# Decayed attention of the last branch: two heads per unit, one unit ahead

## The chip, the cores and the metric

The kernel runs on one core of a Trainium2 chip. The time is that of one execution on the device, in microseconds (us), as the median of several runs. A profile shows one execution, engine by engine: PE is TensorE (PEld its weight loads), DVE the vector engine, ACT the scalar engine, POOL GpSimd, SP the queue that issues most DMAs. The granted clock of TensorE is given as a share of its full 2.4 GHz.

## What is computed

A two-layer block with convolution, state-space and linear attention, cross attention and MLPs is followed by a second block on 512 tokens of width 1024. That second block has three attention branches (a: differential, b: sliding window, c: decayed or "forgetting"), each gated by a projection `gm` and projected up by `w_up`; the sum goes through `w_o` and a last norm. Only branch c is touched. Cut to what matters:

```python
def forgetting_attention(q, k, v, logf):          # S = 512, H = 8, d = 64, nb = 4 blocks of 128 queries
    c = jnp.cumsum(logf, axis=1)
    def one_block(args):
        qblk, cblk, start = args
        s = jnp.einsum('bqhd,bkhd->bhqk', qblk, k) * scale
        decay = jnp.transpose(cblk, (0, 2, 1))[:, :, :, None] - c_k[:, :, None, :]
        s = jnp.where((dist >= 0)[None, None], s + decay, -jnp.inf)
        p = jax.nn.softmax(s, axis=-1)
        return jnp.einsum('bhqk,bkhd->bqhd', p, v)

qc, kc, vc, fc, gc, gm = ...                      # columns of h @ w_in
uc = jnp.einsum('bse,ed->bsd', yc * jax.nn.silu(gc), w_up_c)
merged = gates[:, :, 0] * ua + gates[:, :, 1] * ub + gates[:, :, 2] * uc
out = rms_norm(x + merged @ w_o)
```

## The kernel before, in words

The program is written by hand, engine by engine: each engine has one list of instructions in program order, and semaphores join the lists. Nothing reorders them. Products of the large gemms are made as three products of rounded halves (`product3`, lines 596 to 598), so each step over 128 rows of weights is three records of 128x512. Weights stream through `raw`, are split by ACT into `w_hi` (L1336) and by DVE into `w_lo` (L2157), in four slots.

**Units.** Attention of each branch runs in units. In branches a and b a unit holds two maps (64 rows of `QK` at partitions 0 to 63 and 64 to 127). In branch c a unit is one head `hd` and one block `t` of 128 queries, 32 units; it has (t+1)*128 keys, so its row is 128, 256, 384 or 512 wide. For each unit:

- PE makes the scores (`scores_c`, L1269: 64 rows, (t+1)*128 columns, one product, two records);
- DVE adds the running decay sums of keys and queries (`maxima`, L2860), adds the causal mask on the last block (L2864) and takes the row maximum (L2865);
- ACT takes the exponential and the row sum (`exps`, L2045);
- PE transposes the weights (`turns_c`, L728, one record per 128x128 block), ACT copies them out (L2092), PE multiplies by the values (`values_c`, L1282, 64 columns, two records per block), DVE scales and gates the result (L2901).

**Key sums.** The decay sums of a head's keys are spread over partitions by four transposes on PE (`key_sums`, L728 reading `sm`), and DVE copies them negated (L2918). A head's sums are made in unit 1 of the head before.

**What sets the order.** Function `units` (PE) issues, for a unit n: in c and b the transposes of n, the scores of n+2 (`AHEAD` = 2), steps of the gate projection `gm` as filling (`gate_products`: 64 steps over the whole branch, eight of them before the first unit, the rest spread evenly), and the values product of n. In a (`AHEAD` = 1) the order is scores of n+1, half of the steps, transposes of n, the other half, values of n. DVE goes through reciprocal (L2884), maxima of n+2, at times one weight split, values of n, at times key sums. ACT goes through the copy of n's transposes, the exponentials of n+2, at times a copy of a finished gate chunk (L2072) and a weight split.

**Banks.** Everything but the gemms goes through four PSUM banks `paux`, taken in turn by a fixed list (`aux_plan`): entry number a can only be written when entry a-4 has been read (`next_aux`, `free_aux`). So the order in that list sets who waits for whose reader.

After the 32 units the output of the branch is transposed (`turned_output`), and the gemms `up_c` and `w_o` and the last norm follow; they need all of it.

## Time and profile before

| | us |
|---|---|
| median of 3 runs | 2392.0 (2391.42 to 2392.83) |
| the profiled execution | 2392.23 |
| its span | 2390.5 |
| PE busy | 2280.9 |
| DVE busy | 1312.0 |
| ACT busy | 914.6 |
| DMA, mean rate over the span | 94 GB/s |

The span is what the profile covers of the execution; some 1.7 us lie around it. Busy times of matmul records overlap a little (a record is longer than the distance to the next), so distances are read from start to start in the timeline. Branch c's units lie between 2196 and 2315 us, branch a's, used for comparison, between 1833 and 1907 us.

### The profile page before, as it was taken

Reading aid. Unit: us, or ns where it says so; the run is one execution under the profiler, and the core shown is the slowest. Engines: PE = TensorE matmul, PEld = TensorE weight load, DVE = VectorE, ACT = ScalarE, POOL = GpSimd, SP = SyncE. Lnnn points to the kernel's source line nnn. Section 1 sums busy time; section 2 is a strip of 40 time slices with the busy share of each in tenths; the row PEclk is TensorE's granted clock in tenths of the full one; section 3 lists DMA queues with packets and bytes.
Section 4 is the critical chain, followed back from the end, with each engine's and each line's share of the span. In section 5 each row is a group of like instructions: output and inputs, shape, how many; then the busy total and the mean of one; then the engine's idle time right before and its main releaser. Section 6 shows DMA issues by size and latency. Waiting matters only on the chain.

```text
span 2390.5 us, 27557 instructions
## 1 busy us (share of the span) xinstructions
PE 2280.9 (95%) x11120; PEld 1862.9 (78%) x11120; DVE 1312.0 (55%) x1946; ACT 914.6 (38%) x1636; POOL 164.2 (7%) x115
## 2 busy tenths in 40 slices
PE   7997889999999999999899999999899899999898
PEld 5886677877888888888787778888777688877677
DVE  4997798754833334735564573333533734622564
ACT  3353564342423323334334332232334534523353
POOL 0000300040400000400003040000000000000000
PEclk9998999999999999999899999999989999999999
DMA  5222224423333232321232223332222232122113
GB/s 164 88 88 74 86 93 176 145 80 124 116 106 106 88 106 89 115 71 54 80 141 71 88 91 113 99 106 89 88 106 88 54 88 71 54 88 88 36 36 115
DMA packets 180021, 224.68 MB, mean 94 GB/s; under 512 B 16603, under 2 KB 139174, under 8 KB 178870
## 3 DMA queue, kind: packets, MB, share of 16 engines
q1 hardware_dynamic: 167632, 191.90, 25.2%
q10 hardware_dynamic: 11686, 22.62, 2.7%
q0 software_dynamic: 576, 8.39, 0.9%
q8 instruction: 89, 1.46, 0.3%
q14 instruction: 38, 0.31, 0.0%
HBM read 213.72 MB, written 9.18 MB: 93 GB/s over the span
## 4 chain that ended last, share of the span: by engine, by line
PE 84%; DVE 11%; ACT 2%; issue 2%; POOL 1%; ACTq 1%; DVEq 0%
PE gemm L596 25%; PE gemm L597 24%; PE gemm L598 24%; PE aux L728 2%; DVE w_lo L2157 1%; DVE y_plain L2363 1%; PE aux L971 1%; PE aux L993 1%; PE aux L1269 1%; DVE x_lo L2180 1%; DVE work L2295 1%; POOL work L528 1%; PE aux L1282 1%; PE aux L1239 0%; PE aux L1086 0%
## 5 line engine op out<-in xcount | busy, mean ns | idle before, releaser
L596 PE MATMUL gemm<-x_hi,w_hi 128*128 128x512 f32 x1288 | 518.4, 402 | 6.1 <-DVE w_lo L2157 3.7
L598 PE MATMUL gemm<-x_hi,w_lo 128*128 128x512 f32 x1288 | 504.0, 391 | 0.0
L597 PE MATMUL gemm<-x_lo,w_hi 128*128 128x512 f32 x1288 | 504.0, 391 | 0.0
L2157 DVE TENSOR_TENSOR w_lo<-raw,w_hi 128x1024 fp32r<-128x1024 f32 x222 | 284.7, 1304 | 283.2 <-ACT w_hi L1336 282.4
L1336 ACT ACTIVATE w_hi<-raw 128x1024 fp32r<-128x1024 f32 x222 | 228.4, 1054 | 280.9 <-PE gemm L598 277.8
L596 PE MATMUL gemm<-w_hi,y_hi 128*128 128x512 f32 (+1 forms) x832 | 320.8, 386 | 0.0
L597 PE MATMUL gemm<-w_lo,y_hi 128*128 128x512 f32 (+1 forms) x832 | 317.6, 382 | 0.0
L2153 DVE TENSOR_TENSOR w_lo<-raw,w_hi 128x1024 fp32r<-128x1024 f32 x140 | 168.4, 1222 | 268.8 <-ACT w_hi L1334 259.4
L596 PEld LDWEIGHTS gemm<-x_hi,w_hi 128*128 128x128 f32 x1288 | 243.3, 189 | 82.8 <-issue 24.2
L598 PE MATMUL gemm<-w_hi,y_lo 128*128 128x512 f32 x768 | 299.5, 390 | 0.0
L598 PEld LDWEIGHTS gemm<-x_hi,w_lo 128*128 128x128 f32 x1288 | 243.0, 189 | 52.0
L597 PEld LDWEIGHTS gemm<-x_lo,w_hi 128*128 128x128 f32 x1288 | 243.3, 189 | 47.1 <-issue 1.0
L1334 ACT ACTIVATE w_hi<-raw 128x1024 fp32r<-128x1024 f32 x140 | 144.7, 1054 | 251.8 <-PE gemm L598 246.8
L596 PE MATMUL gemm<-w_hi,x_hi 128*128 128x512 f32 (+2 forms) x640 | 224.7, 351 | 2.1 <-issue 2.1
L597 PE MATMUL gemm<-w_lo,x_hi 128*128 128x512 f32 (+2 forms) x640 | 220.5, 344 | 0.0
L598 PE MATMUL gemm<-w_hi,x_lo 128*128 128x512 f32 (+2 forms) x640 | 220.1, 344 | 0.0
L596 PEld LDWEIGHTS gemm<-w_hi,y_hi 128*128 128x128 f32 x832 | 157.0, 189 | 31.5 <-issue 1.7
L597 PEld LDWEIGHTS gemm<-w_lo,y_hi 128*128 128x128 f32 x832 | 156.8, 189 | 31.6 <-issue 1.7
L598 PEld LDWEIGHTS gemm<-w_hi,y_lo 128*128 128x128 f32 x768 | 144.6, 188 | 30.2
L2363 DVE SCALAR_TENSOR_TENSOR y_plain<-work,par,y_plain 128x512 f32<-128x512 f32 x217 | 148.9, 745 | 4.3 <-ACT y_plain L1540 3.9
L596 PEld LDWEIGHTS gemm<-w_hi,x_hi 128*128 128x128 f32 x640 | 123.0, 192 | 21.9 <-issue 6.9
L597 PEld LDWEIGHTS gemm<-w_lo,x_hi 128*128 128x128 f32 x640 | 123.0, 192 | 14.4 <-issue 0.2
(327 smaller groups left out, 2788.3 us busy)
## 6 DMA issues: line engine op xcount, KB each, us to landing
raw<-in_mlp_w_dram SPq DMA_DIRECT2D x64, 1024.0 KB, 5.4
raw<-in_w_in_dram SPq DMA_DIRECT2D x31, 1024.0 KB, 5.1
raw<-in_odd_w_in_dram SPq DMA_DIRECT2D x12, 1024.0 KB, 5.2
raw<-in_even_w_in_dram SPq DMA_DIRECT2D x10, 1024.0 KB, 4.9
raw<-in_even_w_in_dram SPq DMA_DIRECT2D x16, 512.0 KB, 5.2
raw<-in_xa_w_k_dram SPq DMA_DIRECT2D x8, 1024.0 KB, 5.1
raw<-in_xa_w_v_dram SPq DMA_DIRECT2D x8, 1024.0 KB, 5.1
raw<-in_even_w_out_dram SPq DMA_DIRECT2D x8, 1024.0 KB, 4.9
```

Source lines behind the costliest of these rows:

```text
L528: pool.tensor_scalar(DIAG[:, i % 3, :], ident[:, :], par_col("even_conv_w", i * KC + KC - 1), None, ALU.mult).then_inc(S["diag_ready"], 1)
L596: pe.matmul(dst, a_hi, b_hi, start=first, stop=False)
L597: pe.matmul(dst, a_hi, b_lo, start=False, stop=False)
L598: return pe.matmul(dst, a_lo, b_hi, start=False, stop=last)
L728: return pe.transpose(dst, src, ident[0:src.shape[0], 0:src.shape[0]])
L971: ins = pe.matmul(dst[:, t2 * MEM:(t2 + 1) * MEM], XQ[:, 2 * hd + d, t * P:(t + 1) * P], KT[:, 2 * hd + d, :], start=(d == 0), stop=(d == 1))
L993: ins = pe.matmul(dst[:, :], VM[:, m, j * P:(j + 1) * P], PTX[:, m, hd, :], start=(m == 0), stop=(m == 1))
L1334: act.activation(piece(w_hi, s), raw_piece(n, s % 2), ACT.Copy).then_inc(w_hi_ready, 1)
L1336: act.activation(w_hi[:, s % W_SLOTS, :, :], raw[:, n % RAW_SLOTS, :, (s % 2) * P:(s % 2 + 1) * P], ACT.Copy).then_inc(w_hi_ready, 1)
L2153: dve.tensor_tensor(piece(w_lo, s), raw_piece(s // 2, s % 2), piece(w_hi, s).bitcast(F32), ALU.subtract).then_inc(w_lo_ready, 1)
L2157: dve.tensor_tensor(w_lo[:, s % W_SLOTS, :, :], raw[:, s // 2 % RAW_SLOTS, :, half], w_hi[:, s % W_SLOTS, :, :].bitcast(F32), ALU.subtract)\
L2363: ins = dve.scalar_tensor_tensor(U[:, f, CONV_W - 1:] if last else acc, U[:, f, i:i + T], par_col("even_conv_w", i * KC + f), acc, ALU.mul ...
```

## The change

A unit of branch c now holds two heads `(pr, t)`, 2*pr and 2*pr+1, so there are 16 units of two maps. The two score products of a unit are issued one behind the other on rows 0 to 63 and 64 to 127. Branch c takes the order of branch a: one unit of scores ahead, half of the steps ahead of the transposes and half behind. The transposes of both maps take a bank each, and ACT copies each on its own; the odd units' copies go to `y_plain`. On DVE the adds stay two, while the mask, the maximum and the reciprocal cover both maps in one instruction each; the values step has two writes. Key sums of the next pair's two heads are made behind the values product of units 0 and 1, and are kept in `y_plain` (`KEY_SUMS`), four heads at a time. The gate steps are still 64, eight before the first unit, 3.5 on average in each unit. Branches a and b keep their instructions.

```diff
-AHEAD = dict(a=1, b=2, c=2)
+AHEAD = dict(a=1, b=2, c=1)
...
-            if name == "C" and u[1] == 1 and u[0] + 1 < 8:
-                out += [("cb_c", u[0] + 1)]
             turns = [(name, "T", u, j) for j in range(nt)]
             scores = [(name, "S", us[n + ahead], j) for j in range(ns)] if n + ahead < len(us) else []
             out += turns + scores if ahead == 2 else scores + turns
             if pv:
                 out += [(name, "PV", u)]
+            if name == "C" and u[1] < 2 and u[0] + 1 < 4:
+                out += [("cb_c", 2 * u[0] + 2 + u[1])]
...
-    e += [("fc_rows",), ("fc",), ("cc",), ("cb_c", 0)]
-    e += units("C", [(hd, t) for hd in range(8) for t in range(TT)], 1, 1, True) + [("Ct", j) for j in range(4)]
+    e += [("fc_rows",), ("fc",), ("cc",), ("cb_c", 0), ("cb_c", 1)]
+    e += units("C", [(pr, t) for pr in range(4) for t in range(TT)], 2, 2, True) + [("Ct", j) for j in range(4)]
...
-            return (EX[:, 0, 0, :], EX[:, 1, 0, :], EX[:, 0, 1, :] if b == "b" else NC)[unit_slot(b, u)]
+            return (EX[:, 0, 0, :], EX[:, 1, 0, :], EX[:, 0, 1, :])[unit_slot(b, u)]
+
+        KEY_SUMS = y_plain[:, 2048:4096].rearrange("p (a b) -> p a b", b=T)
+
+        def pair_weights(u, g):
+
+            return PT[:, g, :] if UNIT[("C", u)] % 2 == 0 else y_plain[:, T * g:T * g + T]
...
-                    before(u)
-                    if b == "a":
+                    if b != "b":
                         if n + 1 < len(us):
                             scores(us[n + 1])
                         gate_products(b, (gate_steps(b, n - 1, len(us)) + gate_steps(b, n, len(us))) // 2)
+                    if b == "a":
                         pe.wait_ge(S["p_ready"], UNIT[(name, u)] + 1)
                     else:
                         pe.wait_ge(S["unit_exp"], UNIT[(name, u)] - 2 * TT + 1)
-                    turns(u, next_aux(name, "T", u, 0)).then_inc(aux_done, 1)
-                    if b != "a" and n + 2 < len(us):
+                    for g in range(2 if b == "c" else 1):
+                        turns(u, next_aux(name, "T", u, g), g).then_inc(aux_done, 1)
+                    if b == "b" and n + 2 < len(us):
                         scores(us[n + 2])
                     gate_products(b, gate_steps(b, n, len(us)))
-                    aux_read(pe, name, "T", u, 0)
+                    for g in range(2 if b == "c" else 1):
+                        aux_read(pe, name, "T", u, g)
                     values(u, next_aux(name, "PV", u)).then_inc(aux_done, 1)
+                    after(u)
                 gate_products(b, KC * KC)
                 at["gate"] = 0
                 at["panel"] += 4
...
             def scores_c(u):
-                hd, t = u
-                a = 64 * (hd % 2)
-                pe.matmul(next_aux("C", "S", u, 0)[:, 0:(t + 1) * P], QK[a:a + 64, hd // 2, t * P:(t + 1) * P],
-                          QK[a:a + 64, 4 + hd // 2, 0:(t + 1) * P], start=True, stop=True).then_inc(aux_done, 1)
-
-            def turns_c(u, dst):
-                row = unit_row("c", u)
+                pr, t = u
+                for g in range(2):
+                    a = 64 * g
+                    pe.matmul(next_aux("C", "S", u, g)[:, 0:(t + 1) * P], QK[a:a + 64, pr, t * P:(t + 1) * P],
+                              QK[a:a + 64, 4 + pr, 0:(t + 1) * P], start=True, stop=True).then_inc(aux_done, 1)
+
+            def turns_c(u, dst, g):
+                e = unit_slot("c", u)
                 for kt in range(u[1] + 1):
-                    ins = turn(dst[:, kt * P:(kt + 1) * P], row[:, kt * P:(kt + 1) * P])
+                    ins = turn(dst[:, kt * P:(kt + 1) * P], EX[:, e, g, kt * P:(kt + 1) * P])
                 return ins
 
             def values_c(u, dst):
-                hd, t = u
-                e = UNIT[("C", u)] % 2
-                for kt in range(t + 1):
-                    ins = pe.matmul(dst[:, 0:64], PT[:, e, kt * P:(kt + 1) * P], BV[:, kt, hd * 64:(hd + 1) * 64],
-                                    start=(kt == 0), stop=(kt == t))
+                pr, t = u
+                for g in range(2):
+                    s = slice((2 * pr + g) * 64, (2 * pr + g) * 64 + 64)
+                    for kt in range(t + 1):
+                        ins = pe.matmul(dst[:, 64 * g:64 * g + 64], pair_weights(u, g)[:, kt * P:(kt + 1) * P],
+                                        BV[:, kt, s], start=(kt == 0), stop=(kt == t))
                 return ins
...
-                    if b == "a":
+                    if b != "b":
                         for m in range(2):
                             v = EX[:, e, m, 0:(t + 1) * P]
...
+                    if b == "c":
+                        free_aux(act.activation(pair_weights(u, 0)[:, 0:(u[1] + 1) * P], bank[:, 0:(u[1] + 1) * P],
+                                                ACT.Copy), (B, "T", u, 0))
+                        bank = wait_aux(act, (B, "T", u, 1))
+                        src, dst = bank[:, 0:(u[1] + 1) * P], pair_weights(u, 1)[:, 0:(u[1] + 1) * P]
+                    elif b == "b":
...
-                        row = unit_row(b, u)
-                        bank = wait_aux(dve, ("C", "S", u, 0))
-                        free_aux(dve.scalar_tensor_tensor(row[:, 0:n], EX[:, hd % 2, 1, 0:n],
-                                                          sm[:, 4 + t, hd:hd + 1], bank[:, 0:n], ALU.add, ALU.add),
-                                 ("C", "S", u, 0))
+                        for g in range(2):
+                            bank = wait_aux(dve, ("C", "S", u, g))
+                            free_aux(dve.scalar_tensor_tensor(EX[:, e, g, 0:n], KEY_SUMS[:, 2 * (hd % 2) + g, 0:n],
+                                                              sm[:, 4 + t, 2 * hd + g:2 * hd + g + 1], bank[:, 0:n],
+                                                              ALU.add, ALU.add), ("C", "S", u, g))
                         aux_read(dve, "C", "S", u, 0)
-                        step(dve.tensor_tensor(row[:, n - P:n], row[:, n - P:n], R[:, 0:P], ALU.add))
-                        ins = dve.tensor_reduce(mxs[:, e, 0:1], row[:, 0:n], AX.X, ALU.max, negate=True)
+                        aux_read(dve, "C", "S", u, 1)
+                        last = EX[:, e, :, n - P:n]
+                        step(dve.tensor_tensor(last, last, over(R[:, 0:P], 2), ALU.add))
+                        ins = dve.tensor_reduce(mxs[:, e, 0:2], EX[:, e, :, 0:n], AX.X, ALU.max, negate=True)
...
-                        s = slice(64 * hd, 64 * hd + 64)
-                        ins = dve.scalar_tensor_tensor(YT[:, t, s], bank[:, 0:64], rs[:, e, 2:3], BG[:, t, s],
-                                                       ALU.mult, ALU.mult)
+                        for g in range(2):
+                            s = slice(128 * hd + 64 * g, 128 * hd + 64 * g + 64)
+                            ins = dve.scalar_tensor_tensor(YT[:, t, s], bank[:, 64 * g:64 * g + 64],
+                                                           rs[:, e, 2 + g:3 + g], BG[:, t, s], ALU.mult, ALU.mult)
...
-                    free_aux(dve.tensor_scalar(EX[:, hd % 2, 1, :], bank[:, :], -1.0, None, ALU.mult), ("cb_c", hd))
+                    free_aux(dve.tensor_scalar(KEY_SUMS[:, hd % 4, :], bank[:, :], -1.0, None, ALU.mult), ("cb_c", hd))
...
                 if b == "c":
                     key_sums(0)
+                    key_sums(1)
                 for u in us[:AHEAD[b]]:
                     maxima(u)
                 for n, u in enumerate(us):
-                    weights(u)
+                    if b != "c":
+                        weights(u)
                     if n + AHEAD[b] < len(us):
                         maxima(us[n + AHEAD[b]])
+                    if b == "c":
+                        weights(u)
                     if n:
                         split_chunks(2 * FIRST_PANEL[f"gm_{b}"] + W_SLOTS + gate_steps(b, n - 1, len(us)) // KC)
                     values(u, u == us[-1])
                     if b == "a" and n:
                         gated(n - 1)
-                    if b == "c" and u[1] == 1 and u[0] + 1 < 8:
-                        key_sums(u[0] + 1)
+                    if b == "c" and u[1] < 2 and u[0] + 1 < 4:
+                        key_sums(2 * u[0] + 2 + u[1])
```

What stands in PE's list, before, in the second head: the scores of its unit of 384 columns, one step of the gate, the values product of its unit of 128, the four transposes of the next head's key sums (`ident,sm`), the transposes of its unit of 256 and the scores of its unit of 512.

```order
L1269 MATMUL aux<-work 128x384 [waits aux_free2]
L596 MATMUL gemm<-x_hi,w_hi 128x512
L597 MATMUL gemm<-x_lo,w_hi 128x512
L598 MATMUL gemm<-x_hi,w_lo 128x512
L1282 MATMUL aux<-work 128x64 [waits aux_free3,aux_free1]
L728 MATMUL aux<-ident,sm 128x128 [waits aux_free0]
L728 MATMUL aux<-ident,sm 128x128 x3
L728 MATMUL aux<-ident,work 128x128 [waits aux_free1,unit_exp]
L728 MATMUL aux<-ident,work 128x128
L1269 MATMUL aux<-work 128x512 [waits aux_free2]
```

After, in PE's list at the first pair: the key sums, the two score products of 512 columns, one step, and the transposes of both maps of the unit of 384.

```order
L734 MATMUL aux<-ident,sm 128x128 [waits aux_free0]
L734 MATMUL aux<-ident,sm 128x128 x3
L1279 MATMUL aux<-work 128x512 [waits aux_free1]
L1279 MATMUL aux<-work 128x512 [waits aux_free2]
L602 MATMUL gemm<-x_hi,w_hi 128x512
L603 MATMUL gemm<-x_lo,w_hi 128x512
L604 MATMUL gemm<-x_hi,w_lo 128x512
L734 MATMUL aux<-ident,work 128x128 [waits aux_free3,unit_exp]
L734 MATMUL aux<-ident,work 128x128 x2
L734 MATMUL aux<-ident,work 128x128 [waits aux_free0]
L734 MATMUL aux<-ident,work 128x128 x2
```

Key sums no longer stand right ahead of transposes; the scores come in twos, and a step of the gate stands between scores and transposes.

DVE's list before, where key sums are read: weight split, values, key-sum copy, reciprocal, then the adds, mask and maximum of a unit.

```order
L2157 TENSOR_TENSOR w_lo<-raw,w_hi 128x1024 [waits w_hi_ready]
L2901 SCALAR_TENSOR_TENSOR work<-aux,rs,work 128x64 [waits aux_done]
L2918 TENSOR_SCALAR work<-aux 128x512 [waits aux_done]
L2884 RECIPROCAL rs<-rs 128x1 [waits unit_exp,aux_free3]
L2860 SCALAR_TENSOR_TENSOR work<-work,sm,aux 128x128 [waits aux_done,dve_step]
L2864 TENSOR_TENSOR work<-work 128x128 [waits aux_free0]
L2865 TENSOR_REDUCE mxs<-work 128x1 [waits dve_step]
```

After, at the pair's unit with 512 columns: weight split, the two values writes, key-sum copy, the adds of both maps, then mask and maximum once for both.

```order
L2171 TENSOR_TENSOR w_lo<-raw,w_hi 128x1024 [waits w_hi_ready,dve_step]
L2918 SCALAR_TENSOR_TENSOR work<-aux,rs,work 128x64 [waits aux_done]
L2918 SCALAR_TENSOR_TENSOR work<-aux,rs,work 128x64
L2935 TENSOR_SCALAR y_plain<-aux 128x512 [waits aux_done]
L2874 SCALAR_TENSOR_TENSOR work<-y_plain,sm,aux 128x512 [waits aux_done,aux_free0]
L2874 SCALAR_TENSOR_TENSOR work<-y_plain,sm,aux 128x512 [waits aux_done]
L2880 TENSOR_TENSOR work<-work 128x2x128 [waits aux_free2,aux_free1]
L2881 TENSOR_REDUCE mxs<-work 128x2 [waits dve_step]
L2900 RECIPROCAL rs<-rs 128x2 [waits unit_exp]
```

The reciprocal, which waits for the exponentials of the unit, now stands behind the maximum of the next unit.

## Rows read from the trace of the kernel before

**Rows 1.** The page: span, and the busy times of engines.
```profile
span 2390.5 us, 27557 instructions
...
PE 2280.9 (95%) x11120; PEld 1862.9 (78%) x11120; DVE 1312.0 (55%) x1946; ACT 914.6 (38%) x1636; POOL 164.2 (7%) x115
```
**Rows 2.** Timeline of PE in branch c: start us, us, line, out<-in, count [idle before].
```profile
2196.25 1.09 PE L728 MATMUL aux<-ident,sm 128*128 128x128 f32 x4 [0.28 <-DVE sm L2826]
...
2252.80 1.12 PE L1269 MATMUL aux<-work 64*128 64x512 f32 x2
2253.85 0.50 PE L596 MATMUL gemm<-x_hi,w_hi 128*128 128x512 f32 x1
...
2256.97 0.52 PE L728 MATMUL aux<-ident,work 128*128 128x128 f32 x3 [1.07 <-DVE work L2918]
...
2258.63 0.39 PE L596 MATMUL gemm<-x_hi,w_hi 128*128 128x512 f32 x1
...
2259.32 0.78 PE L1282 MATMUL aux<-work 128*128 128x64 f32 x6
2259.94 0.61 PE L728 MATMUL aux<-ident,work 128*128 128x128 f32 x4
...
2265.49 0.60 PE L728 MATMUL aux<-ident,sm 128*128 128x128 f32 x4
2265.93 0.38 PE L728 MATMUL aux<-ident,work 128*128 128x128 f32 x2
...
2313.51 1.00 PE L1282 MATMUL aux<-work 128*128 128x64 f32 x8
```
**Rows 3.** Waits of PE in branch c, then branch a: us, times, longest us.
```profile
PE aux L728 <- DVE work L2918: 9.2, 7, 2.0
...
PE aux L728 <- DVE work L2878: 4.0, 3, 1.3
```
**Rows 4.** Windows of branch c: length, PE, PEld, DVE, ACT, POOL busy, PEclk, DMA share, GB/s.
```profile
2196.20:2203.00 6.80, 6.75 (x18) 4.91 (x19) 5.28 (x11) 1.09 (x4) 0.00 (x0) 0.51 0.45 137
2230.60:2234.20 3.60, 3.60 (x15) 2.86 (x13) 0.41 (x3) 1.02 (x3) 0.00 (x0) 0.55 0.37 131
```
**Rows 5.** Timeline of PE in branch a.
```profile
1863.56 1.13 PE L1191 MATMUL aux<-work 64*128 64x512 f32 x4
1864.62 0.50 PE L596 MATMUL gemm<-x_hi,w_hi 128*128 128x512 f32 x1
...
1870.96 0.66 PE L728 MATMUL aux<-ident,work 128*128 128x128 f32 x4 [1.32 <-DVE work L2878]
...
1881.29 1.13 PE L1191 MATMUL aux<-work 64*128 64x512 f32 x4
```
**Rows 6.** Windows of the score lines alone, PE and PEld busy, c then a.
```profile
2196.20:2314.60 118.40, 26.29 (x64) 9.88 (x64) 0.96 0.11 36
...
1833.00:1905.00 72.00, 12.96 (x64) 4.82 (x64) 1.00 0.14 44
```
**Rows 7.** Timeline of DVE: branch a, then branch c.
```profile
1865.58 1.28 DVE L2839 SCALAR_TENSOR_TENSOR work<-work,aux 128x512 f32<-128x512 f32 x2
1866.89 1.22 DVE L2842 TENSOR_REDUCE mxs<-work 128x2 f32<-128x1024 f32 x1
...
2251.90 0.29 DVE L2864 TENSOR_TENSOR work<-work 128x128 f32<-128x128 f32 x1
...
2255.94 0.28 DVE L2901 SCALAR_TENSOR_TENSOR work<-aux,rs,work 128x64 f32<-128x64 f32 x1
2256.14 0.68 DVE L2918 TENSOR_SCALAR work<-aux 128x512 f32<-128x512 f32 x1
```
**Rows 8.** Timeline of ACT: branch a, then branch c.
```profile
1868.14 0.72 ACT L2035 ACTIVATE work<-work,mxs 128x512 f32<-128x512 f32 x1 [1.29 <-DVE mxs L2842]
...
1869.48 0.19 ACT L2035 ACTIVATION_READ_ACCUMULATOR work<-work,mxs 128x1 f32 x1
...
2260.58 0.60 ACT L2092 ACTIVATE work<-aux 128x512 f32<-128x512 f32 x1 [1.05 <-PE aux L728]
```

More of the change, by code:

```diff
@@ L206 @@
          + [("B", (hd, t)) for hd in range(4) for t in range(TT)]
-         + [("C", (hd, t)) for hd in range(8) for t in range(TT)])
+         + [("C", (pr, t)) for pr in range(4) for t in range(TT)])
 UNIT = {key: n for n, key in enumerate(UNITS)}
@@ L1144, in gate_products, with units @@
                     at["gate"] += 1
-            def units(b, us, scores, turns, values, before=lambda u: None):
+            def units(b, us, scores, turns, values, after=lambda u: None):
                 name = b.upper()
@@ L1192, in scores_a, with turns_a @@
                               QK[a:a + 64, 4 + hd, 0:(t + 1) * P], start=True, stop=True).then_inc(aux_done, 1)
-            def turns_a(u, dst):
+            def turns_a(u, dst, g):
                 e = UNIT[("A", u)] % 2
@@ L1223, in scores_b, with turns_b @@
                               QK[a:a + 64, 4, lo_key:(t + 1) * P], start=True, stop=True).then_inc(aux_done, 1)
-            def turns_b(u, dst):
+            def turns_b(u, dst, _):
                 row = unit_row("b", u)
@@ L1293, in next_key_sums @@
             def next_key_sums(u):
-                if u[1] == 1 and u[0] + 1 < 8:
-                    key_sums(u[0] + 1)
+                if u[1] < 2 and u[0] + 1 < 4:
+                    key_sums(2 * u[0] + 2 + u[1])
             aux_read(pe, "cc")
             key_sums(0)
-            units("c", [(hd, t) for hd in range(8) for t in range(TT)], scores_c, turns_c, values_c, next_key_sums)
+            key_sums(1)
+            units("c", [(pr, t) for pr in range(4) for t in range(TT)], scores_c, turns_c, values_c, next_key_sums)
             turned_output("Ct", "c", 2)
@@ L2024, in _ @@
                 logs()
-                us = [(hd, t) for hd in range(8 if b == "c" else 4) for t in range(TT)]
+                us = [(hd, t) for hd in range(4) for t in range(TT)]
                 B = b.upper()
@@ L2035, in exps @@
                             ins = act.activation(v, v, ACT.Exp, bias=mxs[:, e, m:m + 1], accum_out=rs[:, e, m:m + 1])
-                    elif b == "b":
+                    else:
                         for g in range(2):
@@ L2091, in _ @@
                         src, dst = bank[:, 0:(u[1] + 1) * P], PT[:, e, 0:(u[1] + 1) * P]
-                    free_aux(act.activation(dst, src, ACT.Copy), (B, "T", u, 0))
+                    free_aux(act.activation(dst, src, ACT.Copy), (B, "T", u, 1 if b == "c" else 0))
                     if n + AHEAD[b] < len(us):
@@ L2883, in weights @@
                     else:
-                        step(dve.reciprocal(rs[:, e, 2:3], rs[:, e, 0:1]))
+                        step(dve.reciprocal(rs[:, e, 2:4], rs[:, e, 0:2]))
                 def values(u, last):
@@ L2917, in key_sums @@
                     bank = wait_aux(dve, ("cb_c", hd))
-                    free_aux(dve.tensor_scalar(EX[:, hd % 2, 1, :], bank[:, :], -1.0, None, ALU.mult), ("cb_c", hd))
+                    free_aux(dve.tensor_scalar(KEY_SUMS[:, hd % 4, :], bank[:, :], -1.0, None, ALU.mult), ("cb_c", hd))
                     aux_read(dve, "cb_c", hd)
-                us = [(hd, t) for hd in range(8 if b == "c" else 4) for t in range(TT)]
+                us = [(hd, t) for hd in range(4) for t in range(TT)]
                 split_chunks(2 * FIRST_PANEL[f"gm_{b}"] + W_SLOTS)
@@ L2924, in _ @@
                     key_sums(0)
+                    key_sums(1)
                 for u in us[:AHEAD[b]]:
```

6 lines of the change are left out of this document (1 added, 5 removed).

## The prediction

> **What bounds the kernel now.** I read the page first. TensorE is busy 2280.9 of 2390.5 us [rows 1], so time can leave only where its own work shrinks or where it stands still. Next the stage that the change touches: it runs from the first key sums at 2196.25 to the end of the last values product at 2313.51 + 1.00 = 2314.51 us [rows 2], which is **118.3 us**. Everything ahead of it keeps its instructions; behind it the gemms of `up_c` and `w_o` wait for this stage's output. So what TensorE's queue saves here, the end saves. The waits of the stage are the third view: TensorE stands 9.2 us in seven waits, all for the vector engine's copy of the key sums [rows 3]. A last view is the granted clock: 6.8 us at the start of the stage ran at 0.51 and 3.6 us from 2230.6 at 0.55 [rows 4], that is mostly at 1.2 instead of 2.4 GHz.
>
> **Part 1, the scores in pairs.** Stage C issues one score product of 64 rows at a time; stage A issues two that stand on the two halves of the rows. In the timeline of C one 64x512 product (two records) starts at 2252.80 and the next work at 2253.85, 1.05 us [rows 2]. In A four records of the same shape, two products, start at 1863.56 and the next work at 1864.62, 1.06 us [rows 5]. The totals agree: 64 records of the same four widths keep TensorE busy 26.29 us in C and 12.96 us in A [rows 6]. The difference is 13.3 us; part of C's figure ran at the low clock, and the ends overlap the next record. From start to start I go by A's total: the pairs take 12.96 us, less 0.07 of overlap (1.12 - 1.05) at each of 16 places, 11.8 us; C's singles take twice that at full clock, so **11.8 us are saved**. Bounds: 0 (the halves take turns) to 13.3.
>
> **Part 2, the waits for key sums.** Before, the key sums of the next head stand between two units; the transposes of the unit after them need the bank of the sums (four banks in turn), and the vector engine reads that bank only behind its values step: 0.28 and then 0.68 us [rows 7], which is the 1.07 us of idle before the transposes at 2256.97 [rows 2]. After, the sums follow a unit's values product, and what reuses their bank is the next unit's second map of transposes. Between stand a pair of scores, two steps of products and the first map's transposes, over 2 us (a step of three products takes 0.69, from 2258.63 to 2259.32 [rows 2]). The vector engine now needs two values writes (0.2 each) and the copy, 1.1 us. All of the **9.2 us** goes; what is late next is part 4's question. Bounds: 0 to 9.2.
>
> **Part 3, switches and clock.** TensorE enters the 64-row form 32 times before, 16 times after. The first large product behind a score lasts 0.50 where others last 0.39 [rows 2]: a switch costs about 0.1 us, and going in and coming out are two. Sixteen fewer pairs of switches give some 3 us at most; sixteen new returns from transposes to products, and the values products that now stand ahead of the scores, take most of it back: **1 us saved**, between 0 and 2. The second low stretch came right behind the early waits, which last up to 2.0 us [rows 3]. Without them I take it to go: 3.6 us at 0.55 did the work of 2.0, **1.6 us saved** (0 to 1.6). The first low stretch follows from what stands before the stage and stays. The TensorE page of the Trainium skill, "TensorE: Matmul & The Clock Gate", Part 4 on transposes, says that transposes do not count as busy for the clock as products do; the denser stage holds the same transposes in less time, so by that rule new low stretches could appear (a rival below).
>
> **Part 4, is one unit ahead enough?** This is the risk of the change. The widest unit (t=3, 512 columns) needs, from the end of its scores: two adds of the key sums, 1.28; the mask on the last block of both maps, which the trace shows only for one map (0.29), so between 0.29 and 0.58, taken in the middle as 0.43, since a fixed part is paid once; one maximum over 1024 elements, 1.22 [rows 7]; two exponentials, from 1868.14 to 1869.67, 1.53 [rows 8]; handovers some 0.3. That is 4.8 us. What TensorE has to do meanwhile, by its new order: one step 0.69, six transposes 0.66 (four of the key sums take 0.44 from 2265.49 to 2265.93, 0.11 each [rows 2]), two steps 1.38, the values product of the unit before, 12 records of 0.103 (six take 0.62 [rows 2]) 1.24, the next scores at least 0.27 (a quarter of 1.06), two steps 1.38: 5.6 us. Covered with 0.8 us left; narrower units have more. The transposes' copies: the first map's four are done 0.44 us after they start, two copies of 0.60 [rows 8] end at 1.64, and the values product comes after eight transposes and two steps, at 2.26: covered with 0.6 us left. The scalar engine's copy of a gate chunk and its split of a weight slot stand behind the exponentials, where the 0.8 us of slack absorbs most of them. So I put this part at **0**, and its price if the cover fails in the rivals. The shared mask, maximum and reciprocal take work off the vector engine, which does not bound. At the end of the stage two values writes instead of one stand before the output's transposes: 0.2 us lost. The last wait for a copy (about 0.5 us) is covered or not.
>
> **The sum.** 11.8 + 9.2 + 1 + 1.6 - 0.2 = 23.4, with the tail's 0.5 up to 23.9 us. A second way, from stage A, which already runs in this order: four of its units take 1881.29 - 1863.56 = 17.73 us [rows 5]. Take out its own wait of 1.32 (it is for a step between exponentials and transposes that C lacks), add what C has more for a pair of heads: two steps 1.4, ten transposes 1.1, twenty values records 2.1, two key sums 0.9. That is 21.9 a pair, 87.6 for four, and 5.5 for the first eight steps and 3.3 for the first low stretch: 96.4, or 21.9 us less than 118.3. Stage A's period holds a few smaller gaps ahead of its transposes, some 0.6 us by my estimate from its sum; if these go too it is 24.3. The three figures lie between 21.9 and 24.3; with one longer values product per unit having one lag less, I take **24.0**. The profiled execution took 2392.23 us (span 2390.5 and 1.7 around it), the median of the runs is 2392.0: 2392.2 - 24.0 = **2368.2 us**, and against the median 2368.0.
>
> **The rivals.** (a) *The cover fails.* The vector engine's mask over two strided blocks, or the scalar engine's chunk copy and split, push the exponentials of the widest unit beyond the 0.8 us. In stage A this unit does wait, 1.32 us at 1870.96 [rows 5], 4.0 us in three waits [rows 3]; the same in each of four pairs costs 5.3, and if waits bring a low stretch back 1.6 more: 2368.2 + 6.9 = 2375.1. The page "TensorEngine Tiling (Array Packing)" of the Trainium skill, Performance Considerations, "PSUM Bottleneck", warns of this: tiling speeds TensorE up but not the reading of its results. Here the reading engines have room on average, so only their latency can bite. (b) *New low-clock stretches*, one like that at 2230.6 in each pair, 1.6 each: 2374.6. Against it: stage A and the steady heads of C stay at full clock with waits of 1.07 to 1.32 us [rows 2, 5]. (c) *The halves don't run together*, so the change doesn't do what it says: for it speaks only that C's operands come from other slots than A's; 2368.2 + 11.8 = 2380.0. (d) *Slower.* One unit ahead with five or six banks needed per unit and four there: if the second map's transposes must wait for the bank of the last values product and the vector engine reads that only behind a weight split that itself waits for the scalar engine, each unit becomes its bare chain. The widest: scores 1.06, vector 2.93, exponentials 1.53, transposes 0.88, copies 1.2, values 1.65, handovers 0.3, 9.55 us; the narrowest some 0.44 of that. Sixteen units average 6.9, 110 us, and with first steps 5.5, low clock 3.3 and key sums 3.5 it is 122.3: 4 us over 118.3, 2396.2. It decides from the point where a values read comes later than the next scores, two steps and a map of transposes, over 2 us after the product; the trace shows the read at 2255.94 right behind a mask and a maximum [rows 7].
>
> **How the numbers follow.** The forecast, 2365 to 2371: 0.66. Rival (a) 0.18, (b) 0.04, (c) 0.07, (d) 0.03, and a gain beyond 27 us 0.02. The range 2364.5 to 2376.5 takes in (a) and (b). About 0.2% (4.8 us) is what a measurement of this kernel can tell from no change. All cases but (d) and a deep form of (a) are faster by more: faster 0.95, within 0.2% 0.02, slower 0.03.
>
> **What would show it.** Part 1: TensorE's busy time on the score line near 13 us. Part 2: no wait of the transposes for the key-sum copy. Part 3: granted clock 1.0 from some 7 us into the stage. Part 4: no wait of transposes for the exponentials, none of the values product for a copy. The stage from key sums to last values should take 94 us. Wrong would be: score line near 25 us (c); waits of over 1 us at each 512-column unit (a); a stage beyond 118 us (d).

## The result, and the profile after

The changed kernel takes **2364.3 us** (median of 4 runs, 2362.35 to 2365.28) against 2392.4 before (4 runs, 2391.42 to 2393.07): the ratio is 0.9882, with a 95% interval of 0.9865 to 0.9899, or 28.1 us less. The forecast was 2368.2 and the lower end of its range 2364.5. So the direction was forecast, and the gain came out 4 us larger than forecast, 0.2 us outside of the range. Two more sets of the same kernel gave 2363.7 and 2364.3.

The profiled execution took 2365.28 us. Its page, which answers to [rows 1]:

```profile
span 2363.5 us, 27477 instructions
...
PE 2264.7 (96%) x11120; PEld 1858.4 (79%) x11120; DVE 1303.8 (55%) x1898; ACT 912.2 (39%) x1636; POOL 164.2 (7%) x115
```

TensorE's busy time fell by 16.2 us and the span by 27.0; the rest was idle time. The stage now runs from the key sums at 2197.12 to the end of the last values product at 2285.61 + 1.89 = 2287.50, **90.4 us** where it took 118.3. It starts 0.9 us later than in the profile of before, so the 27.9 us gained in the stage are 27.0 of span. What stands ahead of the stage is the same in both kernels, and its start differs by about as much between profiles of one kernel (2195.0 to 2197.1 for the changed one, 2196.1 to 2197.4 before).

First the waits of PE in branch c, the view of [rows 3] (us, times, longest), for the kernel after: only three are left, and they stand at the edges of the stage, and none for key sums, exponentials or copies.

```profile
PE aux L734 <- DVEq L2923: 0.7, 1, 0.7
PE aux L1271 <- ACT work L2035: 0.7, 1, 0.7
PE aux L734 <- DVE sm L2840: 0.3, 1, 0.3
```

The windows, as in [rows 4] and [rows 6]. The first two lines are the stage split where the clock came back (length, busy of PE, PEld, DVE, ACT, POOL, PEclk, DMA share, GB/s): 3.6 us at 0.53 and then full clock to the end. The third is the score line alone: 13.27 us busy, where [rows 6] had 26.29.

```profile
2197.10:2200.70 3.60, 3.58 (x15) 2.84 (x16) 3.53 (x5) 0.00 (x0) 0.00 (x0) 0.53 0.00 0
2200.70:2287.50 86.80, 86.80 (x515) 68.97 (x513) 56.29 (x124) 41.73 (x111) 0.00 (x0) 1.00 0.16 49
```

```profile
2197.10:2287.50 90.40, 13.27 (x64) 5.02 (x64) 0.98 0.15 47
```

The timeline of PE through one pair (start, us, line, out<-in, count), to be read against [rows 2]:

```profile
2236.05 1.13 PE L1279 MATMUL aux<-work 64*128 64x512 f32 x4
2237.11 0.50 PE L602 MATMUL gemm<-x_hi,w_hi 128*128 128x512 f32 x1
2237.45 0.39 PE L603 MATMUL gemm<-x_lo,w_hi 128*128 128x512 f32 x1
...
2239.94 1.45 PE L1293 MATMUL aux<-work 128*128 128x64 f32 x12
2241.32 0.49 PE L1279 MATMUL aux<-work 64*128 64x128 f32 x4
...
2243.00 0.39 PE L604 MATMUL gemm<-x_hi,w_lo 128*128 128x512 f32 x1
2243.23 1.04 PE L734 MATMUL aux<-ident,work 128*128 128x128 f32 x8
2244.02 0.47 PE L602 MATMUL gemm<-x_hi,w_hi 128*128 128x512 f32 x1
2244.34 0.39 PE L603 MATMUL gemm<-x_lo,w_hi 128*128 128x512 f32 x1
...
2245.49 1.89 PE L1293 MATMUL aux<-work,y_plain 128*128 128x64 f32 x16
...
2256.81 1.13 PE L1279 MATMUL aux<-work 64*128 64x512 f32 x4
...
2285.61 1.89 PE L1293 MATMUL aux<-work,y_plain 128*128 128x64 f32 x16
```

From the scores of 512 columns to the next such scores it is 2256.81 - 2236.05 = 20.76 us for two heads. Behind four score records of 512 columns the next work starts 1.06 us on, as in stage A [rows 5]. The transposes at 2243.23 start 0.23 us behind the start of the last large product, the usual distance from one large product to the next, so there is no gap. (Such a record lasts 0.39 us, longer than the distance to its successor.)

What the transposes could have waited for, on DVE and then ACT, for the unit of 512 columns: the adds, the mask over both maps, the maximum, then the first and the last piece of the exponentials and the two copies.

```profile
2237.28 1.41 DVE L2874 SCALAR_TENSOR_TENSOR work<-y_plain,sm,aux 128x512 f32<-128x512 f32 x2 [0.43 <-PE aux L1279]
2238.79 0.42 DVE L2880 TENSOR_TENSOR work<-work 128x256 f32<-128x256 f32 x1
2239.25 1.22 DVE L2881 TENSOR_REDUCE mxs<-work 128x2 f32<-128x1024 f32 x1
```

```profile
2240.51 0.72 ACT L2047 ACTIVATE work<-work,mxs 128x512 f32<-128x512 f32 x1 [1.20 <-DVE mxs L2881]
...
2241.84 0.18 ACT L2047 ACTIVATION_READ_ACCUMULATOR work<-work,mxs 128x1 f32 x1
...
2243.87 0.60 ACT L2096 ACTIVATE y_plain<-aux 128x512 f32<-128x512 f32 x1 [0.41 <-PE aux L734]
2244.36 0.59 ACT L2106 ACTIVATE y_plain<-aux 128x512 f32<-128x512 f32 x1
```

The mask takes 0.42 us (forecast 0.43). The exponentials are done at 2241.84 + 0.18 = 2242.02, 1.2 us ahead of the transposes, and the second copy at 2244.95, 0.5 us ahead of the values product at 2245.49.

### The profile page after: what moved, and what is told of

It is laid out like the page before. It is cut to its first block, busy times and chain, and to the rows that moved or that the text cites. A ratio compares the mean times of both kernels' runs of the same rounds, so it can differ in the third digit from the quotient of the medians.

```text
span 2363.5 us, 27477 instructions
## 1 busy us (share of the span) xinstructions
PE 2264.7 (96%) x11120; PEld 1858.4 (79%) x11120; DVE 1303.8 (55%) x1898; ACT 912.2 (39%) x1636; POOL 164.2 (7%) x115
## 4 chain that ended last, share of the span: by engine, by line
PE 85%; DVE 10%; ACT 2%; issue 2%; POOL 1%; ACTq 1%; DVEq 0%
PE gemm L602 25%; PE gemm L604 25%; PE gemm L603 25%; PE aux L734 3%; DVE w_lo L2171 1%; DVE y_plain L2377 1%; PE aux L977 1%; PE aux L999 1%; DVE x_lo L2194 1%; DVE work L2309 1%; POOL work L534 1%; PE aux L1293 1%; PE aux L1279 1%; PE aux L1248 0%; PE aux L1092 0%
## 5 line engine op out<-in xcount | busy, mean ns | idle before, releaser
L2186 DVE CAST y_hi<-work 128x512 fp32r<-128x512 f32 x64 | 34.2, 534 | 181.5 <-ACT work L1848 181.3
```

The costliest lines, as they stand in the source:

```text
L2186: step(dve.tensor_copy(hi, src))
```

## The experiments

The time of the kernel before differed a little from set to set (2392.2, 2393.1 and 2390.6 us), so times are compared within a set, and small differences are read in the stage's own length in the profile. Two lengths serve below: the stage from the key sums to the last values product, and its **clock-free length**, from which I take what the low clock cost (each 0.4 us slice of the stage by 1 - PEclk). It is 88.7 us in the three profiles of the changed kernel and 113.0 to 113.3 in the three of the kernel before. The theory: the two products of a pair run at once on the two halves of the rows, the waits for key sums are gone, and one unit of scores ahead is enough. The rival: the two products take turns, and the new order alone brought the gain.

### 1. Both products on one half

```diff
-                    a = 64 * g
+                    a = 0
```

> The changed kernel, but both score products of a unit read rows 0 to 63, so they share one half of the array; the second head's scores are those of the first head (that part of the result is left out). Theory (the halves run at once, which is worth 16 score products): the score line's busy time rises from 13.3 to about 25 us and the time by 11.8 us, less what slack in the stage swallows (none, since TensorE never waits there), so 2364.3 + 11.8 = 2376. Rival (the gain came from the order and the fewer switches, the pair takes turns anyway): the same time, 2364, and 13.3 us.

Measured: 2373.98 us beside 2363.68 for the changed kernel in the same set, +10.3 (11.8 expected). PE's timeline of the same unit, and the score line's busy time:

```profile
2238.88 1.98 PE L1279 MATMUL aux<-work 64*128 64x512 f32 x4
2240.80 0.50 PE L602 MATMUL gemm<-x_hi,w_hi 128*128 128x512 f32 x1
```

```profile
2194.00:2302.00 108.00, 22.00 (x64) 10.50 (x64) 0.97 0.12 40
```

The pair of 512 columns now takes 1.92 us to the next work instead of 1.06. At the four widths it is 0.86, 0.63, 0.43 and 0.22 us more, 2.14 a pair of heads: **8.6 us** is what running at once is worth. The stage is 100.5 us long, 10.1 more; 1.7 of that is the low clock (7.2 us of it instead of 3.6). The halves do run at once, and the rival falls. But the number was 11.8 in the forecast. A product of 512 columns that stands alone takes 1.05 us [rows 2], and the second one here 0.86: about 0.2 us is paid once for a group, and the second product does not pay it even on the same half. So 3.2 of the 11.8 us belong to the fewer entries and not to the halves.

### 2. The key sums moved, and nothing else

In the kernel before, `("cb_c", hd + 1)` moves behind the values product of the head's first unit, on PE, DVE and in the list of banks:

```diff
-            if name == "C" and u[1] == 1 and u[0] + 1 < 8:
-                out += [("cb_c", u[0] + 1)]
...
+            if name == "C" and u[1] == 0 and u[0] + 1 < 8:
+                out += [("cb_c", u[0] + 1)]
```

> The kernel before, 32 units of one head, two ahead, with one part of the change alone: the key sums of the next head are made behind the values product of a head's first unit instead of ahead of the transposes of its second. Theory: the seven waits (9.2 us) and the second low-clock stretch (1.6 us) go, 2392.4 - 10.8 = 2381.6. Rival (the waits only change their releaser, or the clock falls elsewhere): less than 5 us gained.

Measured: 2380.22 us against 2392.2, **12.0 us** faster. The stage is 107.2 us long, 11.0 less than in the first profile of before; the last 1.0 lies ahead of it, where nothing was changed. Of PE's waits in the stage this is left beside the edges:

```profile
PE aux L1282 <- ACT work L2092: 0.6, 2, 0.3
```

The seven waits are gone, the second low-clock stretch too, and the clock-free length is 103.8 us, 9.3 less than before. So 11 to 12 of the 28 us can be had with a few lines and no pairs. Two heads take 12.17 + 12.18 = 24.35 us here where they are not delayed by a wait for a copy. The two heads that are delayed take 12.71 and 12.72, 1.1 us more together.

The list of waits makes a wait too short. It counts from the end of the record before, and that end lies behind the point where the next work usually starts. The values product ahead of the wait at 2256.97 [rows 2] in the kernel before, and the corresponding product here:

```profile
2255.34 0.56 PE L1282 MATMUL aux<-work 128*128 128x64 f32 x4
```

```profile
2247.83 0.56 PE L1282 MATMUL aux<-work 128*128 128x64 f32 x4
2248.22 0.50 PE L728 MATMUL aux<-ident,work 128*128 128x128 f32 x3
```

Without a wait the transposes start 0.39 us behind it, with the wait 1.63: 1.24 us lost, where the list has 1.07. The five shorter waits cost about 1.2 us each and the two long ones 2.2 each by this measure, **10.5 us** in all and not 9.2. That fits the 9.3 us above, since this kernel also loses 1.1 to its two waits for copies.

### 3. A step between the two products

```diff
                 for g in range(2):
                     a = 64 * g
+                    if g:
+                        gate_products("c", at["gate"] + 1)
                     pe.matmul(next_aux("C", "S", u, g)
```

> The changed kernel with one step of the gate between the two score products of a unit (taken from the steps that followed them): each product enters the 64-row form alone, as before the change, but in the new order and without the key-sum waits. Theory (overlap is worth 8.6 us by the pair on one half, and an entry costs a fixed part of 0.2 us in the score product plus 0.1 in the first large product behind it): stage +8.6 + 16 x 0.3 = +13.4 us, time 2377, plus up to 2 us where the second scores now come too late for the widest unit. Rival (entries are free, what the new order saved beyond the overlap was in waits alone): +8.6, 2372.3.

Measured: 2380.22 us against 2393.1 before in its set, a stage of 106.4 us, 103.0 clock-free: 14.3 more than the changed kernel. PE's timeline of one unit, and the score line:

```profile
2242.64 1.12 PE L1281 MATMUL aux<-work 64*128 64x512 f32 x2
2243.70 0.50 PE L602 MATMUL gemm<-x_hi,w_hi 128*128 128x512 f32 x1
...
2244.59 1.12 PE L1281 MATMUL aux<-work 64*128 64x512 f32 x2
2245.64 0.88 PE L734 MATMUL aux<-ident,work 128*128 128x128 f32 x6
```

```profile
2196.00:2302.50 106.50, 26.31 (x64) 9.83 (x64) 0.97 0.12 40
```

PE waits for nothing inside the stage. A pair of heads takes 24.39 us, 3.63 more than 20.76; 2.14 of it is the overlap (experiment 1), and the other 1.49 is four entries, so **0.37 us an entry** into the 64-row form and out of it, 0.2 in the score product and the rest around it. The expectation for the stage was 13.4 us more at 0.3 an entry; the time came out 3 us above the 2377 expected, 1.7 of it from a low-clock stretch of the longer kind. The rival (free entries, 8.6) falls. The price need not all belong to the 64-row form: the first large product behind scores starts its successor 0.34 us on (2237.11 to 2237.45), behind transposes 0.32 us on (2244.02 to 2244.34), elsewhere 0.23. No run splits a group of products over all rows, so what that would cost is not shown. And 24.39 is what experiment 2 has, 24.35, with the old order. Once the waits are gone the new order in itself is worth nothing; what counts is that the two products stand side by side.

### 4. The cover taken away

Without steps between scores and transposes:

```diff
                         if n + 1 < len(us):
                             scores(us[n + 1])
-                        gate_products(b, (gate_steps(b, n - 1, len(us)) + gate_steps(b, n, len(us))) // 2)
+                        if b == "a":
+                            gate_products(b, (gate_steps(b, n - 1, len(us)) + gate_steps(b, n, len(us))) // 2)
```

> The changed kernel with no step of the gate between the next unit's scores and the transposes: all of a unit's steps stand behind its transposes. Theory (1.2 us of slack before the transposes of the widest unit, which the moved one or two steps of 0.7 use up; two switches fewer per unit, each 0.1): waits of 0.2 to 0.7 us at the four widest units, and 1 to 2 us back from the switches: within 2 us of 2363.7. Rival (the halves of the steps ahead are what covers the chain everywhere): waits at every unit, +8 us or more.

Measured: 2365.48 us beside 2393.1 before, a stage of 91.5, 1.2 more than the changed kernel's. PE's waits in branch c:

```profile
PE aux L734 <- ACT work L2048: 1.6, 4, 0.7
```

Four waits, at the four units of 512 columns, 1.6 us together: their slack of 1.2 us is used up where one or two steps (0.7 each) have left. The stage grew by less than the waits, so some 0.4 us at least come back from switches (changes from one kind of product to another). The other twelve units need no step ahead at all.

### 5. The chain made longer

```diff
+                        for _ in range(2):
+                            step(dve.tensor_reduce(mxs[:, e, 0:2], EX[:, e, :, 0:n], AX.X, ALU.max, negate=True))
                         ins = dve.tensor_reduce(mxs[:, e, 0:2], EX[:, e, :, 0:n], AX.X, ALU.max, negate=True)
```

> The changed kernel with the row maximum of a unit computed three times over: the chain of a unit is longer by 2.4 us at 512 columns, 1.9 at 384, 1.4 at 256 and 0.9 at 128, on the vector engine. Theory (slack of the widest unit 1.2 us, of the others 1.9 and more): the transposes of the four widest units wait 1 to 1.6 us each, the others not, +4 to +7 us, 2368 to 2371. Rival (slack is larger since the vector engine's other work gives way): no change, 2363.7. Rival (one unit ahead was only just enough): waits at most units, +15 us.

Measured: 2377.05 us, 16.0 under the kernel before in its set, where the changed kernel had been 28.5, 28.1 and 26.3 under it in three other sets. The stage, which is read more sharply, is 102.3 us long: **12.0 us lost**. Its waits, and one unit on PE and DVE:

```profile
PE aux L734 <- ACT work L2047: 7.9, 5, 2.1
PE aux L734 <- DVE work L2920: 1.0, 2, 0.5
```

```profile
2239.53 1.13 PE L1279 MATMUL aux<-work 64*128 64x512 f32 x4
...
2241.16 0.39 PE L604 MATMUL gemm<-x_hi,w_lo 128*128 128x512 f32 x1
2242.03 1.05 PE L734 MATMUL aux<-ident,work 128*128 128x128 f32 x6 [0.48 <-DVE work L2920]
...
2247.36 0.40 PE L604 MATMUL gemm<-x_hi,w_lo 128*128 128x512 f32 x1
2249.83 1.09 PE L734 MATMUL aux<-ident,work 128*128 128x128 f32 x8 [2.07 <-ACT work L2047]
```

```profile
2244.03 0.42 DVE L2880 TENSOR_TENSOR work<-work 128x256 f32<-128x256 f32 x1
2244.49 2.48 DVE L2882 TENSOR_REDUCE mxs<-work 128x2 f32<-128x1024 f32 x2
2247.00 1.22 DVE L2883 TENSOR_REDUCE mxs<-work 128x2 f32<-128x1024 f32 x1
...
2248.32 0.48 DVE L2920 SCALAR_TENSOR_TENSOR work<-aux,rs,work 128x64 f32<-128x64 f32 x2
```

The expectation (4 to 7 us) was about half of what was measured. The widest unit does wait, up to 2.1 us, but something else comes with it. The vector engine reads the values products out of their banks behind the longer maximum, and these reads free the banks that the transposes of the next units need (1.0 us for L2920, 0.48 of it at 2242.03). The wait list holds 8.9 us of the 12.0; distances from start to start hold nearly all. The pair from 2239.53 on takes 24.15 us, 3.39 more than 20.76. Of this, 2.24 us are the wait at 2249.83 (2.47 behind the last large product instead of 0.23), 0.64 the wait at 2242.03 (0.87 instead of 0.23), 0.24 the six transposes behind it, which take 0.81 instead of 0.57, and 0.12 the gap ahead of the widest unit's values product. Only this last part can be the scalar engine's copies. A chain of one unit has slack of its own, but the engine that carries it also serves the unit before. The direction of rival (a) of the forecast is thus real: 2.4 us more on the vector engine at the widest unit, 6.6 over the four widths, take nearly half of the gain.

### 6. Two steps ahead in branch a

Branch a runs in the order that branch c now has, and still waits. The edit puts one more of a unit's steps ahead of the transposes:

```diff
-                        gate_products(b, (gate_steps(b, n - 1, len(us)) + gate_steps(b, n, len(us))) // 2)
+                        gate_products(b, (gate_steps(b, n - 1, len(us)) + gate_steps(b, n, len(us)) + (b == "a")) // 2)
```

> The changed kernel, and in branch a two of a unit's three gate steps ahead of its transposes instead of one. There TensorE waits 1.3 us at each unit of 512 columns for the vector engine's combining of the two maps (4 times), with small gaps at other units. Theory: most of the 1.3 us is covered by the moved step of 0.7, the copies behind the transposes then take a part of that back: 2 to 4 us faster, 2360 to 2362. Rival (the values product now waits for the copy what the transposes waited before): no change, 2363.7.

The waits of branch a in the changed kernel and with the edit, from a window that also holds its last unit:

```profile
PE aux L734 <- DVE work L2894: 5.9, 4, 1.9
```

```profile
PE aux L734 <- DVE work L2894: 3.8, 4, 1.4
```

The waits fell by 2.1 us. The time was 2361.99 us, in another set than the changed kernel's 2363.68. So both were run once more on one chip:

> The kernel with two steps ahead of the transposes in branch a once more, beside the changed kernel on the same chip. Theory: its branch a ends 3 us earlier, and in the median it is 2 to 3 us faster, 2361 against 2363.7; if the first stretch of branch c is 7.2 us again it is this kernel's, and the gain shown is 1.7 smaller than branch a's. Rival: within 1 us of the changed kernel.

2363.64 against 2364.29 us, 0.65 less: within the spread of either (2362.9 to 2365.7 and 2363.3 to 2364.6). Both profiles of this kernel have 7.2 us of low clock at the start of branch c, which gives 1.7 us back. Faster than the changed kernel it is not shown to be.

### 7. The clock at the start of the stage

Between the profile of before and that of after, the first low-clock stretch had shrunk from 7.2 to 3.6 us and the second was gone. Is that the change? Both kernels were profiled twice more for it.

> The changed kernel once more, for its profile. If the length of the low-clock stretch at the start of branch c (3.6 us in the first profile of it, 6.8 before) belongs to the change, it is 3.6 again. If it is chance, it lies somewhere between 3 and 7 us. The time 2364.3 within 1.5.

> The kernel before once more, for its profile. If the first low stretch belongs to its order, 6.8 us again, if chance, another length. Theory for the second stretch (it follows the waits of 2.0 us): it is there again near the third unit of the third head; rival: gone or elsewhere. The waits 9.2 us within 0.3.

> The changed kernel a third time, for the low-clock stretch at the start of branch c. So far 3.6 us long in two profiles of it and in two of its variants, 7.2 in all five profiles of kernels that do not run scores in pairs, and 7.2 in the variant with more steps ahead in branch a, whose branch c is word for word the same. If the pairs decide it: 3.6 again, and the 1.7 us between the two lengths belong to the change. If chance does: either. Time 2363.7 within 1.

> The kernel before a third time, for its low-clock stretches in branch c: the first was 7.2 us twice, the second 3.6 and 7.2. If they belong to its order: 7.2 again, and a second one behind the waits of 2 us. If chance: other lengths, or none behind these waits.

In this order they took 2363.7, 2395.2, 2364.3 and 2390.4 us, the kernel before in one run each time.

The low stretches found at the start of branch c and inside it, as start and length in us, in whole slices of 0.4 us. Slices at the edges are low only in part: summed by the granted clock, every 3.6 or 4.0 of this table is 3.4 us of low clock, at a cost of 1.7, and every 7.2 is 6.8, at a cost of 3.4.

| kernel | first stretch | second stretch |
|---|---|---|
| before | 2196.0, 7.2 | 2230.4, 3.6 |
| before, again | 2197.2, 7.2 | 2231.6, 7.2 |
| before, third | 2197.2, 4.0 | 2228.0, 3.6 |
| after | 2197.2, 3.6 | none |
| after, again | 2196.8, 4.0 | none |
| after, third | 2194.8, 3.6 | none |
| both on one half | 2194.8, 7.2 | none |
| key sums moved | 2195.2, 7.2 | none |
| scores split | 2196.0, 7.2 | none |
| steps behind | 2196.4, 4.0 | none |
| three maxima | 2197.2, 3.6 | none |
| two steps ahead in a | 2191.6, 7.2 | none |
| the same, again | 2192.8, 7.2 | none |

Windows of the second profile of before and of the third, so that the lines can be seen (columns as above):

```profile
2197.20:2204.40 7.20, 7.04 (x19) 5.11 (x20) 5.39 (x12) 1.09 (x4) 0.00 (x0) 0.53 0.46 143
2231.60:2238.80 7.20, 7.20 (x25) 5.46 (x23) 1.72 (x6) 1.69 (x5) 0.00 (x0) 0.53 0.21 74
```

```profile
2197.20:2201.20 4.00, 4.00 (x11) 2.98 (x10) 3.83 (x9) 0.49 (x2) 0.00 (x0) 0.57 0.34 80
2228.00:2231.60 3.60, 3.60 (x15) 3.12 (x14) 0.98 (x4) 0.49 (x2) 0.00 (x0) 0.53 0.65 225
```

The **second** stretch goes with the waits for key sums: three of three profiles with them have it, each time behind the second wait of 2.0 us, and none of ten without. Experiment 2 moves the key sums and nothing else, and its one profile has neither the waits nor the stretch. But a long wait alone does not bring it: the kernel with three maxima has two waits of 2.1 us, 24 us apart where the two of before are 14, and no low stretch behind either. What more it needs is not shown. The **first** is not settled. It has two lengths, the kernel before shows both, and so chance has a part in it; but pairs have the short one five times in seven and the other kernels only once in six. What decides it stays open. The difference is worth 1.7 us.

## Why the prediction was outside of its range

By the clock-free lengths and the experiments, the 27.9 us between the two profiles are:

| | forecast | measured |
|---|---|---|
| scores at once on two halves | 11.8 together | 8.6 (experiment 1) |
| fewer entries into the 64-row form | with the line above, and 1 for switches | 5.9 (experiment 3: 16 x 0.37) |
| waits for key sums | 9.2 | 10.5 (experiment 2, from start to start) |
| low clock | 1.6 | 3.4 |
| end of the stage and rest | -0.2 to 0.3, and 0.6 taken on top | -0.5 |
| sum | 24.0 | 27.9 |

The row for the end and the rest is what the others leave. They come from different profiles, so half a microsecond there is no more than their error.

**Part 1** (scores in pairs) gave the right total: the score line's busy time is 13.27 us against the 12.96 of [rows 6] on which it rested. Its reason was half right: 8.6 us are the halves, 3.2 the second product's missing fixed part.

**Part 3** is the step that failed, in both its terms. The switches were put at 1 us because new returns from transposes to products were thought to take most of the gain back. Splitting the pairs shows 0.37 us an entry, of which the score line holds 0.2: sixteen entries are 2.7 us outside of the score line, not 1. That is close to the forecast's own figure before it took anything off ("some 3 us at most"). Nothing was taken back: with 32 entries each, the new order takes 24.39 us a pair of heads and the old one 24.35 (experiments 3 and 2). The low clock was put at 1.6 us since the first stretch was said to stay; in the profiles of after only half of it stayed. The clock gave 3.4 us, 1.8 more than forecast, and partly by chance: had the first stretch been of the longer kind, the time would have been about 2366, inside the range.

**Part 2** was right in its mechanism: moving the key sums alone removes the seven waits. Its size was taken from the list of waits, 9.2 us, and was 1.3 us too small, since from start to start these waits cost 10.5 (experiment 2).

**Part 4** was right: no wait for exponentials or copies. The slack was computed as 0.8 us and measured as 1.2, that of the copies as 0.6 and 0.5. From the end of the scores at 2237.11 TensorE has 6.12 us to do before the transposes at 2243.23, not 5.6. The next scores take 0.42 us and not a quarter of 1.06, and steps take 0.80 and 1.49 us behind scores, alone and in twos, where 0.69 and 1.38 were counted.

**The second way**, from stage A, gave 21.9 us for a pair of heads; it is 20.76. I had left 0.6 us of small gaps in, and charged the additional transposes and records at their full distance although they join runs already open. It held the estimate at 24.0 when the terms from stage C, with the switches and the waits at their real price, lead to 26.4, and with the clock's to 28.2. Neither of the two ways gave more than 24.3. The bounds were too narrow as well: at the upper bound of every part (13.3, 9.2, 2 and 1.6) the sum is 26.4, still less than the 28.1 measured, because the switches (bound 2, measured 2.7), the waits (9.2, 10.5) and the clock (1.6, 3.4) all lay outside of theirs.

Of the **rivals**, (c) fell by experiment 1, and (d) never came near: the vector engine's read of the values product of the widest unit starts at 2247.42, 0.04 us behind the end of its product (2245.49 + 1.89), and that of the unit before at 2241.50, 0.11 behind (2239.94 + 1.45). These are the two rows of DVE:

```profile
2241.50 0.48 DVE L2918 SCALAR_TENSOR_TENSOR work<-aux,rs,work 128x64 f32<-128x64 f32 x2 [0.95 <-PE aux L1293]
...
2247.42 0.48 DVE L2918 SCALAR_TENSOR_TENSOR work<-aux,rs,work 128x64 f32<-128x64 f32 x2 [2.62 <-PE aux L1293]
```

(a) did not happen, but experiments 4 and 5 show that its place was right: the widest unit is the first to wait, and one or two steps fewer, or 2.4 us more of vector work, bring it about. (b) did not appear in any profile of the new order: the stage holds full clock once it is up, with 16.8 us of transposes in 90. Part 4 of the page "TensorE: Matmul & The Clock Gate" of the Trainium skill says that transposes do not count as busy for the clock in the way that products do. At this share of transposes the trace shows no low clock that could come from it. The section "PSUM Bottleneck" of the page "TensorEngine Tiling (Array Packing)" of the Trainium skill warns that copies out of the banks may bind once tiling has made TensorE faster. Here they did not: the second copy was done 0.5 us ahead of the values product.

## What to carry to other kernels

Put products that use part of the rows side by side, even where nothing can overlap: each separate entry into the partial form costs a fixed price (0.37 us here), which comes on top of what the halves save by running at once (0.86 us for a 512-column pair in f32). When banks are handed out in turn, look for a bank whose reader stands, on its own engine, behind work for another product: moving the key sums alone was worth 11 to 12 us. Read what a wait costs from start to start, with a stretch without the wait beside it: the list of waits was nearly 0.2 us short at each. And when one stage serves as a model for another, test the model on that stage's own gaps before it is allowed to pull the sum down.

## What had not been expected of the hardware

Low-clock stretches near the start of branch c come in two lengths, 3.4 and 6.8 us by the granted clock, in the same kernel from one execution to the next, at a cost of 1.7 or 3.4 us. The difference alone moves the time of this kernel by 0.07%, and differences of that size between two kernels can't be read from one profile each. A second f32 product of 64 rows on the same half costs 0.86 us for 512 columns, while the first costs 1.06.
